# Expert gates of a two-block transformer layer: one-hot matmuls for tiles 0-55, an indirect scatter through DRAM for tiles 56-127

## The reference, cut to what matters

```
q = (xb @ w_query).reshape(t, 8, 2, 128)
scores = einsum("thpc,hpkc->thpk", q, sk)          # 8 heads, 2 halves, 128 keys
s1, i1 = top_k(scores[:, :, 0], 16)
s2, i2 = top_k(scores[:, :, 1], 16)
cand = s1[..., :, None] + s2[..., None, :]         # 16 x 16 per head
cand_idx = i1[..., :, None] * 128 + i2[..., None, :]
top_s, top_pos = top_k(cand, 16)
gate = softmax(top_s)
act = gelu(einsum("td,thkd->thk", xb, expert_down[idx]))
out = einsum("thk,thkd->td", gate * act, expert_up[idx])
```

## Time and profile before

| | |
|---|---|
| median of 3 runs | 1501.67 us (1500.6 to 1502.99) |
| profiled execution, span | 1499.1 us, 32502 instructions |
| TensorE (PE) busy | 1423.8 us, 95% of the span |
| VectorE (DVE) busy | 1107.4 us, 74% |
| ScalarE (ACT) busy | 689.6 us, 46% |
| GpSimd (POOL) busy | 25.0 us, 2% |
| moved by DMA | 223.04 MB, mean 149 GB/s |

### The profile page before, as it was taken

How to read it: one execution, slowest core, us unless ns; L and a number is a source line. 1 busy time by engine, 2 the same in 40 slices (tenths; PEclk the granted TensorE clock), 3 DMA queues, 4 the chain that set the end, 5 groups by cost and what they waited for, 6 DMA issues and landing times.

```text
span 1499.1 us, 32502 instructions
## 1 busy us (share of the span) xinstructions
PE 1423.8 (95%) x12164; PEld 1392.5 (93%) x12164; DVE 1107.4 (74%) x1975; ACT 689.6 (46%) x1012; POOL 25.0 (2%) x15
## 2 busy tenths in 40 slices
PE   6999999999699999999999999999998998999986
PEld 6998899999699999999999999999988897999986
DVE  6775737999968888888899996555576667666665
ACT  5823456667453333333333334444454444444434
POOL 0000000000500000000000000000000000000000
PEclk9999999999899999999999999999999998999998
DMA  5320344455254334443444434555554224555532
GB/s 214 127 99 1 143 169 145 166 194 181 99 197 141 140 140 140 142 146 135 143 147 148 147 140 147 189 175 189 176 194 153 101 97 157 172 195 173 193 113 85
DMA packets 31311, 223.04 MB, mean 149 GB/s; under 512 B 3553, under 2 KB 3681, under 8 KB 4497
## 3 DMA queue, kind: packets, MB, share of 16 engines
q1 hardware_dynamic: 30528, 218.22, 41.3%
q0 software_dynamic: 720, 3.97, 0.8%
HBM read 221.13 MB, written 1.05 MB: 148 GB/s over the span
## 4 chain that ended last, share of the span: by engine, by line
PE 82%; DVE 10%; issue 3%; ACT 3%; DMA 2%; ACTq 0%; DVEq 0%; SPq 0%
PE ps L348 24%; PE ps L349 23%; PE ps L350 23%; PE ps L762 6%; DVE wlo L344 3%; DMA raw<-in_wts 1%; ACT whi L331 1%; DVE h L491 1%; PE ps L456 1%; DVE i L1441 1%; DVE sc L1438 1%; DVE sq L428 1%; PE ps L704 0%; PE ps L623 0%; DVE alo L512 0%
## 5 line engine op out<-in xcount | busy, mean ns | idle before, releaser
L344 DVE TENSOR_TENSOR wlo<-raw,whi 128x1024 fp32r<-128x1024 f32 x412 | 502.2, 1222 | 168.8 <-ACT whi L331 164.6
L331 ACT ACTIVATE whi<-raw 128x1024 fp32r<-128x1024 f32 x412 | 435.2, 1058 | 403.9 <-PE ps L350 354.9
L348 PE MATMUL ps<-ahi,whi 128*128 128x256 f32 x2016 | 586.0, 291 | 28.3 <-DVE wlo L344 12.7
L349 PE MATMUL ps<-alo,whi 128*128 128x256 f32 x2016 | 574.0, 285 | 0.0
L350 PE MATMUL ps<-ahi,wlo 128*128 128x256 f32 x2016 | 573.5, 284 | 0.0
L348 PEld LDWEIGHTS ps<-ahi,whi 128*128 128x128 f32 x2016 | 391.4, 194 | 36.2 <-issue 27.1
L349 PEld LDWEIGHTS ps<-alo,whi 128*128 128x128 f32 x2016 | 390.6, 194 | 0.3 <-issue 0.2
L350 PEld LDWEIGHTS ps<-ahi,wlo 128*128 128x128 f32 x2016 | 390.2, 194 | 0.0
L348 PE MATMUL ps<-phi,whi 128*128 128x256 f32 x1200 | 342.7, 286 | 1.6 <-DVE plo L1560 1.6
L349 PE MATMUL ps<-plo,whi 128*128 128x256 f32 x1200 | 339.0, 282 | 0.0
L350 PE MATMUL ps<-phi,wlo 128*128 128x256 f32 x1200 | 338.3, 282 | 0.0
(11 more groups left out here) (321 smaller groups left out, 963.0 us busy)
## 6 DMA issues: line engine op xcount, KB each, us to landing
raw<-in_wts SPq DMA_DIRECT2D x206, 1024.0 KB, 4.8
cst<-in_c POOLq DMA_DIRECT2D x1, 1216.0 KB, 12.6
x<-in_x_t SPq DMA_DIRECT2D x1, 1024.0 KB, 5.0
kk<-in_keys POOLq DMA_DIRECT2D x1, 1024.0 KB, 5.1
out_dram<-h SPq DMA_DIRECT2D x4, 256.0 KB, 2.5
cs<-in_c POOLq DMA_DIRECT2D x1, 960.0 KB, 5.1
wp<-in_w_pool POOLq DMA_DIRECT2D x1, 256.0 KB, 13.0
pt<-in_ple_t POOLq DMA_DIRECT2D x1, 256.0 KB, 5.8
```

Of the source, the lines that this page charges most:

```text
L331: nc.scalar.activation(whi[:, j, :], raw_tile(j // 2, j % 2), ACT.Copy).then_inc(s["w_hi"], 1)
L344: nc.vector.tensor_tensor(wlo[:, j, :], raw_tile(j // 2, j % 2), whi[:, j, :].bitcast(F32), ALU.subtract).then_inc(s["w_lo"], 1)
L348: nc.tensor.matmul(out_ap, wh, xh, start=first, stop=False, skip_group_check=True)
L349: nc.tensor.matmul(out_ap, wh, xl, start=False, stop=False, skip_group_check=True)
```

## The change

- The top-k runs head by head (candidates, choose, locate, weigh), beginning in the query pass as soon as a head's two scores are there. spend adds up estimated times of VectorE's steps and issues a wlo for each 1.66 us (BEAT). GpSimd's two multiplications go; VectorE does them head by head. The exponential is one per head, before the tiles in EXP_AT.
- locate also computes an address spot = (i1*128 + i2)*256 + token for each of the 16 choices.
- GpSimd's queue zeroes a DRAM tensor gates_dense (16384 x 256 words) in four parts, behind projection tiles 2, 6, 10 and 14. For each head it issues 32 indirect DMAs, each of which adds 128 gates (one per partition) to 128 words of that tensor; a head waits until the one before has landed. Behind them it reads the gates of tiles 56-127 back in 18 loads of four tiles (512 KB), into two buffers gd.
- One-hot groups cover tiles 0-55 alone (SPLIT): 64 groups of 12 matmuls with 56 columns a token. They stand before down tiles 80-127, two, one and one (GROUPS_OF). TensorE's transposes stand after tile 76 instead of 60.
- In the up pass VectorE multiplies each of tiles 56-127 by its gates from gd, two tiles before its phi; no group is left there.
- The working buffers of the top-k move to the space of x and pf, which are free from the query pass on.

```diff
-EVERY_A, EVERY_B = 8, 4
-CHOSEN_AT = 60
-CV_AT = 48
+BEAT = 1.66
+EXP_AT = (0, 8, 20, 28, 40, 48, 60, 72)
+SPLIT = 56
 GT = 4
 N_GROUPS = T // GT
+CHOSEN_AT = 76
+GROUPS_AT = 80
+GROUPS_OF = (2, 1, 1)
...
@@ -303,15 +316,40 @@
...
+            blank = pf[:, :, :].rearrange("p a t -> p (a t)")
+            nc.gpsimd.memset(blank, 0.0).then_inc(s["zero_ok"], 1)
+            pl.wait_ge(s["zero_ok"], 1)
+            rows_ = dense.rearrange("(p a b) o -> p a (b o)", p=P, b=2 * T)
+            n_rows = rows_.shape[1] // 4
+            for part in range(4):
+                pl.wait_ge(s["evac"], 4 * part + 2)
+                pl.dma_start(rows_[:, part * n_rows:(part + 1) * n_rows, :], m3(blank, n_rows)).then_inc(s["zeroed"], 16)
...
-            pl.dma_start(iota16[:, :], c1[:, 12 * P + PG * T:13 * P + PG * T]).then_inc(s["keys_in"], 16)
-            for half_, e in ((0, eq0), (1, eq1)):
-                pl.wait_ge(s["key_eq"], half_ + 1)
-                nc.gpsimd.tensor_tensor(e[:, :, :, :], e[:, :, :, :],
-                                        i16s[:, :, half_, :].unsqueeze(2).to_broadcast([P, TB * NH, TOPK, TOPK]),
-                                        ALU.mult).then_inc(s["key_mul"], 1)
...
+            pl.wait_ge(s["seeded"], 1)
+            pl.wait_ge(s["norm_h"], 8)
+            pl.dma_start(count[:, :], c1[:, 12 * P + PG * T:13 * P + PG * T + TB]).then_inc(s["count_in"], 16)
+            pl.wait_ge(s["zeroed"], 64)
+            for h in range(NH):
+                pl.wait_ge(s["pick"], h + 1)
+                if h:
+                    pl.wait_ge(s["scat"], 16 * TB * TOPK * h)
+                for tb in range(TB):
+                    for k in range(TOPK):
+                        pl.indirect_dma_start(
+                            out=dense, out_offset=bass.IndirectOffsetOnAxis(ap=spot[:, tb, h, k:k + 1], axis=0),
+                            in_=gate[:, tb, h, k:k + 1], in_offset=None, compute_op=ALU.add).then_inc(s["scat"], 16)
+            pl.wait_ge(s["scat"], 16 * TB * TOPK * NH)
+            by_tile = dense.rearrange("(n p t) o -> p n (t o)", p=P, t=T)
+            for quad in range(SPLIT // 4, N_EXP // 4):
+                n = quad - SPLIT // 4
+                pl.wait_ge(s["g_mul"], N_GROUPS + (4 * (n - 1) if n >= 2 else 0))
+                pl.dma_start(gd[:, n % 2, :, :], by_tile[:, 4 * quad:4 * quad + 4, :])\
+                  .then_inc((s["gd0"], s["gd1"])[n % 2], 16)
...
+            for n in range(CHOSEN_AT, GROUPS_AT):
+                pe.wait_ge(s["w_lo"], W_EXP + n + 1)
...
+                if n == CHOSEN_AT:
+                    pe.wait_ge(s["pick"], NH)
                     for q in range(3):
...
+                            picks = (key[:, 0, tb], key[:, 1, tb], gate[:, tb])[q].rearrange("p h k -> p (h k)")
...
                 for t in range(GT):
                     for part in range(3):
-                        m = tm(bank(2 + j, half, base=t * half), oh2[:, j, :, t], oh1[:, j, part, :, t],
+                        m = tm(bank(2 + j, SPLIT, base=t * SPLIT), oh2[:, j, :, t], oh1[:, j, part, :, t],
                                start=part == 0, stop=part == 2)
...
+            def gated_steps(i, first=False):
+                g = 0
+                for n in range(12):
+                    for _ in range(GROUPS_OF[n % 3]):
+                        pe.wait_ge(s["oh1"], i * 16 + (g + 1))
+                        if not first or g >= 2:
+                            pe.wait_ge(s["g_mul"], i * 16 + (g - 1))
+                        gate_group(g % 2)
+                        g += 1
+                    pe.wait_ge(s["w_lo"], i * 12 + (W_EXP + GROUPS_AT + n + 1))
+                    pe.wait_ge(s["gelu"], i * 12 + (GROUPS_AT + n - 1))
+                    hidden(n % 4, n % 2)
...
-            with pe.Fori(0, N_EXP // 8 - 1) as i:
+            with pe.Fori(0, N_EXP // 4) as i:
                 for n in range(4):
                     pe.wait_ge(s["w_lo"], i * 4 + (W_UP + n + 1))
                     pe.wait_ge(s["p_split"], i * 4 + (n + 1))
                     add_outer(n, phi[:, n % 2, :], plo[:, n % 2, :])
-                    pe.wait_ge(s["oh1"], i * 4 + (N_GROUPS + n + 2))
-                    pe.wait_ge(s["g_mul"], i * 4 + (N_GROUPS + n))
-                    gate_group((n + 1) % 2)
...
+                    if gated:
+                        act.wait_ge(s["g_mul"], quad * 4 + (N_GROUPS - SPLIT + n + 1))
...
+                act.wait_ge(s["cv_ready"], h + 1)
+                A(cv[:, h % 2, :, :], cv[:, h % 2, :, :], ACT.Exp).then_inc(s["cv_exp"], 1)
+                until = EXP_AT[h + 1] if h + 1 < NH else CHOSEN_AT
+                with act.Fori(EXP_AT[h] // 4, until // 4) as i:
+                    for n in range(4):
+                        gelu(n, i)
+            for n in range(CHOSEN_AT, GROUPS_AT):
...
+            hi_for(W_UP - 1)
+            p_hi(0)
+            act.wait_ge(s["w_used"], W_UP)
+            A(row_of(N_EXP - 1), bank((N_EXP - 1) % 2, T), ACT.Gelu).then_inc(s["gelu"], 1)
+            split_hi(act, W_UP + LEAD, (W_UP + LEAD) % 4)
...
+            def spend(us):
+                spent[0] += us
+                if spent[0] >= BEAT:
+                    spent[0] -= BEAT
+                    next_tile()
...
+            def candidates(h):
+                dve.wait_ge(s["scores"], 2 * h + 2)
+                top16(lambda k: v16[:, k[0], k[1], :], lambda k: i16[:, k[0], k[1], :],
+                      lambda k: sc[:, k[0], 2 * h + k[1], :], [(tb, c) for tb in range(TB) for c in range(2)], 0.28)
+                ch(V.tensor_tensor(cand4, over_k(v16[:, :, 0, :]), over_j(v16[:, :, 1, :]), ALU.add))
+                spend(0.7)
...
+            def choose(h):
+                best = cv[:, h % 2, :, :]
+                top16(lambda tb: best[:, tb, :], lambda tb: ci[:, tb, :], lambda tb: cand[:, tb, :], [0, 1], 0.42)
+                ch(V.tensor_copy(gsum[:, 0, :], best[:, :, 0]))
+                V.tensor_tensor(best, best, b3(gsum[:, 0, :], TOPK), ALU.subtract).then_inc(s["cv_ready"], 1)
+                assert at[0] - W_EXP <= EXP_AT[h], (h, at[0] - W_EXP)
+                spend(0.3)
...
+            def locate(h):
+                V.tensor_copy(i16f[:, :, :, :], i16[:, :, :, :])
+                V.tensor_scalar(cj[:, 0, :, :], ci[:, :, :], 4, None, ALU.logical_shift_right)
+                ch(V.tensor_scalar(cj[:, 1, :, :], ci[:, :, :], 15, None, ALU.bitwise_and))
+                ch(V.tensor_copy(cf[:, :, :, :], cj[:, :, :, :]))
+                spend(0.5)
+                if h == 0:
+                    dve.wait_ge(s["count_in"], 16)
+                    dve.wait_ge(s["zeroed"], 64)
...
+                    ch(V.tensor_tensor(eq3, b3(cf[:, c, :, :].rearrange("p b k -> p (b k)"), TOPK),
+                                       m3(count[:, 0:TOPK], TB * TOPK), ALU.is_equal))
+                    spend(0.7)
+                    ch(V.tensor_tensor(eq[:, :, :, :], eq[:, :, :, :], over_j(i16f[:, :, c, :]), ALU.mult))
+                    spend(0.7)
+                    ch(V.tensor_reduce(out=key[:, c, :, h, :], in_=eq[:, :, :, :], op=ALU.add, axis=AX.X))
+                    spend(0.7)
+                where = cf[:, 0, :, :]
+                ch(V.scalar_tensor_tensor(where, key[:, 0, :, h, :], float(P), key[:, 1, :, h, :], ALU.mult, ALU.add))
+                V.scalar_tensor_tensor(spot[:, :, h, :], where, float(T), b3(count[:, P:], TOPK), ALU.mult, ALU.add)
+                spend(0.3)
...
+                assert at[0] - W_EXP > EXP_AT[h], (h, at[0] - W_EXP)
+                dve.wait_ge(s["cv_exp"], h + 1)
+                soft = cv[:, h % 2, :, :]
+                ch(V.tensor_reduce(out=gsum[:, 1, :], in_=soft, op=ALU.add, axis=AX.X))
+                ch(V.reciprocal(gsum[:, 2, :], gsum[:, 1, :]))
+                V.tensor_tensor(gate[:, :, h, :], soft, b3(gsum[:, 2, :], TOPK), ALU.mult).then_inc(s["pick"], 1)
+                spend(0.5)
...
+            for h in range(NH):
+                candidates(h)
+                if h:
+                    weigh(h - 1)
+                choose(h)
+                locate(h)
+            next_tile(max(0, W_EXP + EXP_AT[NH - 1] + 1 - at[0]))
+            weigh(NH - 1)
+            assert at[0] <= W_EXP + CHOSEN_AT, at[0] - W_EXP
+            next_tile(W_EXP + CHOSEN_AT + 1 - at[0])
...
+            def hidden_steps(i, last=False):
+                base = W_EXP + GROUPS_AT + LEAD
+                g = 0
+                for n in range(12):
+                    split_lo(dve, None, (base + n) % 4, i * 3 + (base + n) // 4)
+                    for _ in range(GROUPS_OF[n % 3]):
+                        if not last or g + 2 < 16:
+                            lay_out(g + 2, i)
+                        apply_gates(g, i)
+                        g += 1
...
+            def apply(n, oct_):
+                dve.wait_ge((s["gd0"], s["gd1"])[n // 4 % 2], (oct_ + (n // 8 - OCT + 1)) * 16)
+                e = oct_ * 8 + n
```

(28 more changed lines are left out.)

377 lines of the change are left out of this document (129 added, 248 removed).

## The result

The changed kernel takes 1476.09 us (median of 4, 1474.95 to 1477.09) beside 1501.53 us for the kernel before (1500.6 to 1503.0): 0.9829 of the time, with an interval of 0.9815 to 0.9843. It is faster, and inside the range, but by 25.4 us where 63.9 were forecast. The profiled span is 1473.1 us, 26.0 less than before; the forecast in spans was 1435.2.

The account below looks back on a forecast made before the run. TensorE, busy 95% of the span, was taken as the bound, with one hole near 400 us. Terms -50.6 - 15.7 + 1.1 - 0.7 + 2 = -63.9 us gave 1437.8 us from 1501.67; range 1428 to 1490.

Parts of the forecast that it names:

- (5): 256 scatters on GpSimd's queue, 1 to 2 us each where 2.08 is allowed, hidden before the up pass: 0.
- rival A: Scatters end late and up tile 54 waits: 256 x (cost - 2.08), 1571 us at 2.6 each; chance 0.15.
- Rival C: Scattered words slow the expert passes' weight loads to 8.6 us: 25 us more, 1463 us; chance 0.10.
- Rival B: GpSimd's index reads hold up VectorE in the top-k stage: 1468 us at 0.3 each, 1511 at 0.6; chance 0.11.
- (1): Gate groups on TensorE fall from 128 to 64: 50.6 us off, with nothing taken for 56 columns instead of 64.
- (3): Engine waits cost 0; gated tiles covered, VectorE 10.5 us against TensorE's 11.8 per three; up-pass handover of 0.7 us goes.
- (2): TensorE's hole near 400 us, from GpSimd's multiplications, goes: 15.7 us off; VectorE's lateness 4 us for 2.9, +1.1.
- (4): Zero fill of 16.8 MB behind projection tiles lengthens weight loads meanwhile: nothing to 12 us, 2 taken.

Follow-up runs that it names:

- run 3: The changed kernel with the one-hot gate matmuls covering tiles 0 to 63 (SPLIT 64 instead of 56): 1459.1 us.
- run 8: Changed kernel with a semaphore per token half and SPLIT 64, plus VectorE's wlo moved behind the gate groups in down steps: 1439.23 us.
- 12: Changed kernel, SPLIT 56, with a semaphore per token half, zero fill after the projections, wlo behind gate groups, and head 0's exponential and gates earlier: 1430.64 us.
- run 7: Changed kernel with a semaphore per token half and SPLIT 64, plus the zero fill held back until the projections are over: 1443.6 us.
- run 1: The changed kernel with every second scatter left out, so half of the chosen experts get no gate: 1441.7 us.
- experiment 5: The changed kernel with wlo computed from raw alone (one input instead of two, values wrong): one run, 1428.86 us.
- 6: The changed kernel with each scatter writing 64 words instead of 128, gates of half the tokens missing: one run, 1442.85 us.

## Why the prediction was right and wrong, point by point

**(5), the scatter: wrong, and the step that failed.** I wrote that each may take 2.08 us and took 1 to 2, "because only the issue is repeated". From the first start (249.20) to the last end (854.05) are 604.85 us, which the page adds up: 493.3 busy, 85.9 between scatters, 25.7 in seven waits for a landing. Without the landings that is 2.26 us each. The undisturbed price, 1.54 + 0.30 = 1.84, was in my range: 249.2 + 256 x 1.84 + 25.7 = 746 us, and 752 with the way of the gates to VectorE, 75 before they are wanted. What the sum had no place for is the 0.39 us, on the mean, that VectorE's running instruction adds (99.1/256); the rest, under 0.04, is the six pauses. The formula of rival A was right: with what the trace gives for the point of decision, (826.8 - 6.2 - 249.2 - 25.7)/256 = 2.13 us, it says 256 x (2.26 - 2.13) = 33 us, and the stop is 33.5. So rival A happened, at a size that takes half of the gain and not all. I had also left out the read of gd itself (4.3 us), and counted one landing of 4.8 per head for which seven of 3.7 on the mean came. Head 0 started at 249.2 us where I had 243, and its gates were wanted at 826.8 where I had 817 (and 817 - 243 is 574, not 572): the two nearly cancel. So that the time lies inside the range is no merit of the mechanism: the range reached to 1490 to hold C, half of B and a fifth of A, and it was this fifth of A, 0.03 of the chances, that came. That is luck.

**Rival B: right place, wrong victim.** I priced index reads that hold up VectorE. The row that I had against it, a plain DMA issue beside a wlo of 1.23 us, told of VectorE's time only, and of a DMA that reads no indices. The scatter is the one that waits, up to 1.05 us, and since the queue was on its way to being the bound, the wait counted. The wait itself is shown, at each scatter; that it is the reading of the indices that waits is argued, from 24 plain issues of GpSimd in twelve of the kernels (the loads of kk and cs) that start beside a wlo with 0.84 to 1.13 us to run: they take 0.54 to 0.58 us, and like ones beside nothing 0.53 to 0.55.

**(1), the gate groups: the total nearly right, for two wrong reasons that cancel in part.** 50.6 us were forecast, 47.1 came: 48 tiles in 192.3 us are 138.2 for the tiles and 54.1 for 64 groups, 101.1 before. I had taken nothing for 56 columns in place of 64; they gave 4.9 us (run 3, and 8 against 12 the same 188.5 - 183.4 = 5.1). The step "a quarter of the columns costs half the time, so columns don't set it" doesn't follow: a fixed part and a part by columns fit the same two rows. The other way, 8.4 us (54.1 + 4.9 - 50.6) went to the second group of each double step; run 8 gives 8.7 back.
The rule of the Trainium skill that I had put beside it ("TensorE: Matmul & The Clock Gate", section "Wait — 56ns, not 53.3ns?", a fixed cost of about 62 ns in one decode mode; which mode ran here no trace shows) doesn't hold for these matmuls: 0.077 us less for 12 of them with 8 columns fewer is 6.4 ns each. And from the start of 12 of them in the kernel after to that of the next product are 0.64 us, 53 ns each:

```profile
570.18 0.82 PE L799 MATMUL ps<-oh,oh 128*128 128x56 bf16 x12
570.82 0.36 PE L386 MATMUL ps<-ahi,whi 128*128 128x256 f32 x1
```

**(3), the waits: wrong for the double steps.** "VectorE 10.5 us of TensorE's 11.8: covered" is true of throughput and says nothing of order. VectorE has 30 us of slack in the stage's 188 (157.62 busy) and is still late 16 times, because what TensorE wants stands behind what waits for ScalarE. Run 8 shows it, by order alone.

**(2), the hole: right.** 378 to 412 us has TensorE busy for 33.57 of 34 us, 21.85 before. The lateness of the whole top-k stage is 4.7 us, where I left 4.

**(4), the zero fill: the mechanism right, 2 us taken, 3.3 found** (at 110 us the kernel is 3.3 late); moving the fill behind the projections gives 3.2 us back (run 7). The weight loads issued meanwhile took 9.6 us, twice the usual 4.8, and ScalarE waited for raw 8.0 us up to 150 us, 3.8 before.

**Rival C** did not happen: with half of the words in DRAM the passes ran no faster (run 1), and the weight loads issued between 250 and 420 us took 4.9 us, 4.8 before.

Added up, against the forecast: +33.5 to +34.1 for the stop, +3.5 for the groups, +2.0 for the start, +0.7 for the lateness, less the 2.4 unassigned: 37.9 us, the distance of the spans. The up pass's stop is nine tenths of it.

## What to carry to other kernels

A queue that is nearly saturated needs a sum of its own: start, count times (busy + gap + what other engines add to it), landings, and the moment when its end is wanted. Price each instruction of it beside what the neighbour runs, not alone; and when it is the bound, move its start, take its round trips out, or put off the moment of need. Each of these gave back eight to nine tenths of its own length here (15.0 of 16.65 us, 26.2 of 32.8, 22.3 of 27.9).

Where an engine does several things in one step, ask first what the others wait for and put it ahead: busy shares say whether there is time, never whether it comes in order.

## What the runs showed of the hardware that I had not expected

An indirect DMA of 128 single words occupies GpSimd for 1.54 us and 0.30 to the next; for 64 words it is 1.41, so by an estimate from these two points (1.28 + 0.002 per word) few large ones would be cheaper than many small ones; larger ones weren't tried. When it starts at least 0.05 us behind a TENSOR_TENSOR on VectorE whose inputs both lie in SBUF, it ends later by that instruction's remaining time less 0.12 us, if more than that remains (1268 cases beside a wlo in eleven kernels, all but the first of each, up to 1.05 us in the kernel after; and 326 of 330 beside others). Beside a TENSOR_TENSOR that takes one input from PSUM it isn't longer (147 cases in the same kernels with over 0.25 us to run, one of them in the kernel after), nor beside a MAX8, FIND_INDEX8 or TENSOR_REDUCE (14 cases in the kernel after). The one-input TENSOR_SCALAR of experiment 5 blocks it as well. Two such instructions can fall into step with each other: 2.57 + 0.30 us against tiles of 2.88 kept one blocked scatter in nearly each tile of the up pass, and in the two kernels with another length (experiments 5 and 6) that was gone.
